# One dot product of distance instead of two: where VectorE adds its own expert rows in a PEER decoder trunk

## The reference

```python
experts = jnp.take_along_axis(cand_idx, pos, axis=-1)      # 8 heads x 16 experts per token
gate = jax.nn.softmax(best, axis=-1)
u = u_tab[experts]
v = v_tab[experts]
act = jax.nn.gelu(jnp.einsum('td,thkd->thk', xb, u))
return jnp.einsum('thk,thkd->td', gate * act, v)
```

## Time and profile before

| | |
|---|---|
| runs | 3195.41, 3194.78, 3188.77 us; median 3194.78 |
| the profiled execution | 3188.19 us, of it 3186.2 us from the first to the last instruction |
| busy | PE 2762.6 us (87%), DVE 2217.6 (70%), ACT 1519.7 (48%), POOL 1291.1 (41%) |
| DMA | 1194.57 MB, mean 375 GB/s; gathers 1073.81 MB, 82.3% of the 16 engines' time |
| TensorE clock granted | mean 0.951 |
| chain that ended last | PE 45%, DMA 25%, DVE 13%, ACT 10%, issue 4% |

### The profile page before, as it was taken

One profiled execution on the slowest core, in us unless ns is written; L12 is line 12 of the kernel. 1 busy time (PEld: TensorE's weight loads), 2 busy tenths in 40 slices (PEclk: granted clock), 3 DMA queues, 4 the chain that ended last, 5 costly groups with the idle time before them and its releaser, 6 DMA issues.

```text
span 3186.2 us, 30486 instructions
## 1 busy us (share of the span) xinstructions
PE 2762.6 (87%) x8496; PEld 1495.5 (47%) x8496; DVE 2217.6 (70%) x5544; ACT 1519.7 (48%) x4079; POOL 1291.1 (41%) x1254
## 2 busy tenths in 40 slices
PE   7888888889998899899999898989999888878887
PEld 6545555444464455455455455545445422223222
DVE  0317456888665887888876788888876777676764
ACT  1424333678343555656443455565544444444443
POOL 0004333453443454544543444445543454434432
PEclk9778999999999999999999899999999999999999
DMA  7009899988999999999999999999999999999997
GB/s 278 14 1 368 346 367 385 413 331 337 404 419 422 425 392 385 391 374 386 406 420 418 420 417 387 362 395 384 401 417 419 409 426 427 427 425 414 427 427 330
DMA packets 217417, 1194.57 MB, mean 375 GB/s; under 512 B 21536, under 2 KB 77856, under 8 KB 79520
## 3 DMA queue, kind: packets, MB, share of 16 engines
q0 software_dynamic: 147456, 1073.81, 82.3%
q1 hardware_dynamic: 69792, 118.83, 10.1%
HBM read 1189.38 MB, written 2.10 MB: 374 GB/s over the span
## 4 chain that ended last, share of the span: by engine, by line
PE 45%; DMA 25%; DVE 13%; ACT 10%; issue 4%; POOL 2%; SPq 1%; POOLq 0%; DVEq 0%; ACTq 0%
PE ps L1745 23%; DMA region_g<-in_uv_dram,experts 18%; DMA region_a<-in_keys_dram 8%; DVE region_g L1255 6%; PE ps L1575 5%; PE ps L1607 3%; PE ps L1636 2%; PE ps L1539 1%; PE ps L1339 1%; ACT L882 1%; ACT x_res L889 1%; POOL region_g L635 1%; PE ps L1604 1%; PE ps L1653 1%; PE ps L1499 1%
## 5 line engine op out<-in xcount | busy, mean ns | idle before, releaser
L1745 PE MATMUL ps<-region_g,x_res 128*128 128x512 f32 x3712 | 1813.2, 621 | 260.6 <-ACT x_res L889 229.4
L635 POOL DMA_INDIRECT region_g<-in_uv_dram,experts x1024 | 1168.3, 1141 | 1645.3 <-PE ps L1745 1344.5
L1255 DVE CUSTOM_DVE_ANT_0 region_g<-region_g,region_h 128x1024 f32<-128x1024 f32 x1024 | 1256.1, 1230 | 503.6 <-DMA region_g<-in_uv_dram,experts 491.2
L1745 PEld LDWEIGHTS ps<-region_g,x_res 128*128 128x128 f32 x3712 | 690.7, 196 | 1089.9 <-issue 571.1
L882 ACT ACTIVATE region_a<-region_a 128x1 f32<-128x1 f32 x1024 | 206.0, 201 | 1245.3 <-DVE region_a L1255 1238.8
L889 ACT ACTIVATE x_res<-ident,region_a 128x128 f32<-128x128 f32 x928 | 372.6, 402 | 30.3
L883 ACT ACTIVATE region_a<-region_a,gate 128x1 f32<-128x1 f32 x1024 | 301.6, 295 | 33.3
L1575 PE MATMUL ps<-region_a 128*128 128x256 f32 x1024 | 253.7, 395 | 49.9 <-DMA region_a<-in_keys_dram 48.7
L1575 PEld LDWEIGHTS ps<-region_a 128*128 128x128 f32 x1024 | 201.2, 198 | 125.5 <-DMA region_a<-in_keys_dram 54.9
L882 ACT ACT_TABLE_LOAD x128 | 164.2, 1283 | 13.2 <-DVE region_a L1255 11.1
L1604 PE MATMUL ps<-region_a 128*128 128x256 f32 x512 | 135.7, 396 | 1.0 <-DVE region_a L1091 1.0
(11 more groups left out here) (228 smaller groups left out, 2324.7 us busy)
## 6 DMA issues: line engine op xcount, KB each, us to landing
region_a<-in_w_q_dram SPq DMA_DIRECT2D x32, 1024.0 KB
region_a<-in_w_odd_dram SPq DMA_DIRECT2D x32, 1024.0 KB
region_g<-in_uv_dram,experts POOLq DMA_INDIRECT x1024
region_g<-in_w_even_dram SPq DMA_DIRECT2D x8, 1024.0 KB, 8.0
region_a<-in_w_even_dram SPq DMA_DIRECT2D x8, 1024.0 KB
region_a<-in_w_out_o_dram SPq DMA_DIRECT2D x8, 1024.0 KB
region_a<-in_keys_dram SPq DMA_DIRECT2D x32, 128.0 KB
region_g<-in_w_out_e_dram SPq DMA_DIRECT2D x4, 1024.0 KB, 8.1
```

Source lines behind the costliest of these rows:

```text
L635: g.indirect_dma_start(out=gath[:, s % NBUF, :], out_offset=None, in_=uv[s // (2 * PHASE)], in_offset=bass.IndirectOffsetOnAxis(ap=experts ...
L1255: v.tensor_tensor_reduce(out=u_, in0=u_, in1=XNr[n // P_HEADS % 3], scale=1.0, scalar=0.0, op0=ALU.mult, op1=ALU.add, accum_out=dots[:, c: ...
L1745: i = t.matmul(PS[:, j, :], diag[:, pe_n(s) % NBUF, :], gath[:, s % NBUF, D_MODEL + j * 512:D_MODEL + (j + 1) * 512], start=first, stop=last)
```

## The change

`row_added` is called one dot product behind the row's own instead of two. Nothing else differs: the same instructions, the same waits, the same 96 rows.

```diff
@@ -1292,8 +1292,8 @@
             for s in range(SLOTS):
                 n, k = s // TOPK, s % TOPK
                 dot_product(s)
-                if s >= 2 and on_dve(s - 2):
-                    row_added(s - 2)
+                if s and on_dve(s - 1):
+                    row_added(s - 1)
                 if s % BLOCK == 2 and s > BLOCK:
                     block_out(s // BLOCK - 1)
                 if k < 7:
```

## The result

The changed kernel takes 3199.27 us (median of 20 runs) against 3192.69 us for the kernel before (20 runs): a ratio of 1.0021, with 95% of 1.0012 to 1.0029. That is 6.6 us slower, 3.8 to 9.3 by the interval, a step that sits right at the 0.2% that can be told from no change. The profiled execution has a span of 3193.7 us.

What follows compares the result with a forecast made beforehand. The gathers' DMA transfer was taken to bound the kernel almost everywhere, TensorE and ScalarE the attention. Terms -3.6 + 6.0 = +2.4 us on the 3194.78 us median gave 3197 us, no change that can be told; range 3184 to 3211.

Steps and rivals of the forecast that it cites:

- the sum: Whole kernel: 3.6 us gained in DMA pauses and 6.0 us lost in the attention, +2.4 us in all.
- The signs for "right": GpSimd's add wait more than halves, moving to TensorE's rows; VectorE waits 30 to 45 us for L883; attention 2 to 8 longer.
- the coupling of VectorE to ScalarE: Sign for wrong: attention growing by over 10 us would show late weights cost more than two rows and a half.
- the term of the late weights: Attention, slots 109 to 173: adds wait for ScalarE's L883, pushing VectorE's work back; 2.45 + 2.45 + 1.1 = 6.0 us lost.
- The rows from 723 to 784 us: Later part of the attention: TensorE has work queued, which hides late pieces; no loss counted.
- The gain: Sooner adds shorten DMA pauses ended by gathers that waited for an add: 1.5 + 1.5 + 0.6 = 3.6 us.
- The three pauses behind adds: DMA pauses of 1.6, 2.3 and 0.6 us ending with a gather that waited for an add; 3.6 us gained.
- in all other places the gather only stands longer in the queue: worth nothing: Outside three DMA pauses, sooner gathers gain nothing, since the backlog covers them, some 6 us in the median case.
- The k = 7 and 15 rows: Their dot products reach TensorE 1.28 us later, 12 delayed at once; taken as nothing, bounds 0 and 2.6 us.
- The attention pays more: Rival, slots 109 to 173: all nine late weights push 2.45 us each; +18 us, 3213 us; chance 0.25.
- The ring gains: Rival: eight gather buffers set the pace, so freeing them sooner closes pauses outside the attention; -17 us, 3178 us; chance 0.15.
- slab loads: Rival: sooner gathers delay key transfers TensorE waits for, 5.6 us, 3203 us in all; chance 0.05.

Runs made afterwards that it cites:

- attention at two, The best kernel: Against the kernel before: adds one dot product behind everywhere, but two behind in slots 104 to 176; 3183.47 us, ratio 0.9977.
- before again: The kernel before, every add two dot products behind, written in the experiments' form and profiled a second time; one run, 3195.72 us.
- end of the slot: Against the kernel before: all 96 adds one dot product behind, but after the slot's ranking, coefficients and mixers' pieces; 3203.47 us, ratio 1.0035.
- only k = 13: Against the kernel before: only rows 109, 125, 141, 157 and 173 one dot product behind, all else two; one run, 3192.96 us.
- attention alone at one: Against the kernel before: the nine adds of slots 104 to 176 one dot product behind, the other 87 two; 3203.4 us, ratio 1.0046.
- attention at zero: Against the kernel before: the nine adds of slots 104 to 176 directly behind their own dot product, the rest two behind; 3225.13 us, ratio 1.0101.
- the kernel with phase 0's edges at one: Against the kernel before: rows below slot 104 and from 181 to 253 one dot product behind, all else two; 3194.74 us, ratio 1.0017.
- the kernel at zero there: Against the kernel before: adds outside slots 104 to 176 directly behind their own dot product, inside two behind; 3235.37 us, ratio 1.0133.

## Why the prediction was right, and where its working was not

The forecast, 3197 us and no change, stands 2 us from the 3199.27 measured, and in part this is luck: its base, the median of three runs, lay 2.1 us above the 3192.69 of twenty, and the gap of 6.6 us between the kernels is well over the 2.4 us of the sum. Both of the sum's terms were too small, that of the loss by more. The signs for "right" came as far as the waits go: GpSimd's wait for the adds fell by more than half, TensorE's rows took it over, and VectorE stood 41.2 us (in 12 rows, 13 were forecast). But the attention grew by 12 us, and over 10 was to show that the coupling of VectorE to ScalarE is dearer than two rows and a half. It is.

**The attention: 6.0 us, measured 12.** The failed step is the term of the late weights. Its parts were right: VectorE stands where and as long as forecast (4.62 us at slot 141, 3.67 at 133). In the sum's own terms: the k = 13 rows alone brought 4.5 us, near the 2.45 + 2.45 of the sum; it is the k = 5 rows, 1.1 us in the sum, that bring some 7.7 us more once both are late (240.0 to 247.7 us). What the term left out is what TensorE does when its wait gets longer. The slots 96 to 176, from the stretches shown and the same view of the others; the last column is the stretch less TensorE's busy time:

| kernel | adds there | us | TensorE busy | clock | rest |
|---|---|---|---|---|---|
| attention at two | two | 233.9 | 211.85 | 0.98 | 22.1 |
| before | two | 235.8 | 212.60 | 0.98 | 23.2 |
| before again | two | 237.6 | 217.04 | 0.96 | 20.6 |
| end of the slot | one, last | 239.9 | 213.74 | 0.97 | 26.2 |
| only k = 13 | k = 13 at one | 240.0 | 215.16 | 0.96 | 24.8 |
| changed | one | 247.8 | 220.31 | 0.94 | 27.5 |
| attention alone at one | one | 247.7 | 220.65 | 0.94 | 27.1 |
| attention at zero | zero | 268.5 | 226.22 | 0.91 | 42.3 |

From two to one (the mean of three against that of two) the rest grows by 5.3 us, near the 6.0 of the sum, but TensorE's own busy time for the same 641 to 643 matmuls grows by 6.7 us, as its granted clock falls from 0.98 or 0.96 to 0.94. The five other profiles at two and near the usual clock have 212.5 to 214.4 us of TensorE in 234 to 236. One such fall can be followed. TensorE of the changed kernel behind slot 133 (start, length, [idle before]):

```profile
693.82 1.55 PE L1499 MATMUL ps<-region_a 64*128 64x384 f32 x4
697.51 1.11 PE L1513 MATMUL ps<-ident,region_a 128*128 128x128 f32 x4 [2.14 <-ACT region_a L750]
698.42 6.08 PE L1745 MATMUL ps<-region_g,x_res 128*128 128x512 f32 x8
```

and of the kernel with only k = 13 at one, where row 133 is at two:

```profile
687.59 1.55 PE L1500 MATMUL ps<-region_a 64*128 64x384 f32 x4
689.99 0.66 PE L1514 MATMUL ps<-ident,region_a 128*128 128x128 f32 x4 [0.84 <-ACT region_a L750]
690.48 3.60 PE L1746 MATMUL ps<-region_g,x_res 128*128 128x512 f32 x8
```

The wait for L750 is 2.14 us instead of 0.84, 1.3 us more (1.1 were forecast for this row). Then the four transposes take 1.11 us for 0.66 and the eight products 6.08 for 3.60: 2.9 us more, over twice the wait itself. The clock of the changed kernel there:

```profile
694.00:696.00 2.00, 1.37 (x4) 0.49 (x4) 1.88 (x6) 0.91 (x3) 1.80 (x2) 1.00 0.98 369
...
698.00:700.00 2.00, 2.00 (x5) 1.10 (x5) 1.97 (x4) 1.73 (x6) 1.08 (x1) 0.50 0.95 348
700.00:702.00 2.00, 2.00 (x4) 0.84 (x3) 1.97 (x5) 1.99 (x4) 0.00 (x0) 0.50 0.98 369
```

0.50 is the lower of its two levels, 1.2 of 2.4 GHz. At this place the kernels split cleanly: 2.14 us of waiting in the changed one and the one with the attention alone at one, eight products in 6.08 and 6.15 us; 4.94 us at zero, 5.23 us; and 0.84 or 0.85 us with 3.60 in all ten other profiles that have row 133 on VectorE. So here the longer wait and the fall come together. But a wait of this length doesn't always bring a fall. The kernel before and its second profile are one program, and near the start of the stretch both have a wait of TensorE of 2.1 us and then one of 2.91 us, both for ScalarE's L889. The first profile and then the second, around the first of these waits:

```profile
584.00:592.00 8.00, 4.96 (x12) 1.77 (x11) 5.78 (x17) 4.56 (x13) 3.46 (x3) 1.00 1.01 428
```
```profile
585.00:593.00 8.00, 5.86 (x11) 1.93 (x9) 5.76 (x17) 4.68 (x13) 2.59 (x3) 0.79 1.01 427
```

The clock stayed up in the one and fell in the other, and likewise at the second wait. In slots 96 to 176 the lower level lasts 10 to 14 us in seven of the eight profiles at two and 20 us in the second profile of the kernel before, 27 us in both at one, and 48 us at zero. As TensorE is busy for most of that time and needs twice as long, half of the difference is about the 6.7 us; no run held the clock, so this is arithmetic. The Trainium skill, page "TensorE: Matmul & The Clock Gate", section "HAM oscillation — how this bites in real kernels", describes this: waits between bursts of matmuls throw the engine back to the slower clock, and the next burst pays. The trace agrees at row 133 (2.14 us of waiting, then 6.08 us for 3.60), and shows equal waits of 2.91 us with and without a fall.

The rows from 723 to 784 us, said to be hidden by TensorE's queue, are not free, but cheap: from slot 144 on the delay grows by 4.4 us more (7.6 to 12.0), over the four rows 149 to 173, and two of the clock's falls (0.83 in 720 to 730 us and again in 800 to 810 us) lie in it.

**The gain: 3.6 us, measured 4 to 8.** The three pauses behind adds are indeed gone. In the changed kernel other pauses stand in slots 256 to 384, behind TensorE's rows; two of them:

```profile
1308.90:1310.10 1.20, 1.20 (x11) 1.12 (x10) 1.20 (x3) 0.44 (x2) 0.40 (x1) 1.00 0.42 123
1318.30:1319.00 0.70, 0.70 (x4) 0.43 (x3) 0.30 (x2) 0.49 (x3) 0.00 (x0) 1.00 0.55 94
```

Where the gain lies can be followed in pieces of eight slots from slot 256 to 384. Slots 304 to 312 take 23.2 to 23.3 us in six kernels that keep row 301 at two (25.0 in a seventh) and 21.1 us in the changed one and the two with phases 1 and 2, or rows 301 and 557, at one. Slots 328 to 336 take 24.4 to 25.6 and 22.8 us. Together 4 to 5 us; the whole stretch, 372.9 to 373.7 us in these three kernels against 377.3 to 383.5 in six at two, has up to 5 us more, most of it in slots 256 to 280, where like kernels differ by as much (64.8 to 68.7 us). The slots from 384 to 512 may give 1 more, phase 2 none. The best kernel spoils the picture: it has its rows there at one too, and its profile shows 22.5 and 24.6 us in the two pieces and 378.2 in the stretch. So of its 7.4 us only the sign and the size are measured, not the place.

So the term was a little small, 3.6 for 4 to 8, and what it was made of was wrong: not mainly the three pauses. Two pauses of 4.1 and 2.9 us (at 1185.5 and 1934.9 us) were each longer than any of the three, and were left out because the gathers that end them, 310 and 566, had not themselves waited for an add. They had waited for GpSimd's L601, and that for the gather before it, which had waited for the add of row 301 or 557. The step that failed is "in all other places the gather only stands longer in the queue: worth nothing". It took GpSimd for an engine that only feeds a queue, and overlooked that its own mixers' pieces stand behind the waiting issue: the question that I had asked of VectorE, not asked of GpSimd. 2.2 us are shown to be that, at row 301; the rest of the gain is not.

**The k = 7 and 15 rows, 1.28 us later, taken as nothing:** small, not nothing. New pauses of the DMA engines stand behind slots 135, 343, 599 and 615, all k = 7, of 0.35 to 0.6 us each, 1.9 us in all, inside the 2.6 us that bounded it.

**The balance:** +12 in the attention and -4 to -8 in phase 1 make +4 to +8 us, for the 3.8 to 9.3 us measured. The 5.4 us of the kernel with phase 0's edges at one have no place in it and stay open.

**The rivals.** "The attention pays more" (+18) was about half right: +12 there, though not by nine rows that each push 2.45 us, but by some 5 us of idle time and 7 of slower matmuls. "The ring gains" (-17) had the right sign outside the attention and less than half of the size. But the kernel at zero there (+42 us) shows that those stretches do feel VectorE's order, which my reading of the DMA share had ruled out, and far more when it is late than when it is early. Whether the ring of buffers or the rows that come late to TensorE carry that, no run tells apart. The wait for keys went from 103.7 to 98.9 us, so slab loads were not held up.

## What to carry to other kernels

Moving an instruction ahead on an engine that works in order moves its wait ahead too: price the wait together with everything that it now holds up, on that engine and on each engine whose own compute stands behind an issue that waits for it. Where one place has a late operand and the others have not, choose the distance by place: two in the attention and one elsewhere beat both kernels, by 7.4 and about 15 us. And do not take a DMA share near 1 as proof that nothing else counts; compare the GB/s of two kernels over the same work.

## What was not expected of the hardware

A stall of TensorE of 2.14 us, in place of 0.84, was followed by its clock at the lower level and by 2.9 us of extra matmul time, so a microsecond of new waiting cost three in all. Elsewhere in the same stretch one program had stalls of 2.1 and 2.91 us without a fall in one profile and with one in the other, so like executions differ in length by such falls. The DMA engines showed a share of 0.96 over a stretch that was 5.8% too long (394.4 against 372.9 us), where the share of the shorter one was 0.99.
